# A 1 MB weight piece loaded by sixteen DMAs of 8 partitions instead of one of 128

## The chip, the cores and the metric

The kernel runs on one core of one Trainium2 chip. The metric is the device time in microseconds (us) of one execution; several executions are timed and their median is compared. TensorE (PE) multiplies matrices, VectorE (DVE) and ScalarE (ACT) work on elements, and SyncE (SP) here does nothing but issue DMAs, which sixteen DMA engines carry out.

## The reference

One layer of a decoder with 256 tokens of width 1024, all in float32. What matters here is its mixture of experts, which takes most of the time and nearly all of the data:

```python
def moe_ffn(h, w_router, b_router, w1, b1, w2, b2):      # 32 experts, top 4
    ...
    def expert_block(acc, xs):
        tok, g, e = xs
        u = jnp.dot(h_pad[tok], w1[e], ...) + b1[e]       # w1[e]: 1024 x 2048, 8 MB
        y = jnp.dot(clamped_swiglu(u), w2[e], ...) + b2[e]  # w2[e]: 1024 x 1024, 4 MB
        return acc.at[tok].add(y * g[:, None]), None
```

Before it stand the input projection, four retention heads, eight attention heads and the output projection; behind it a last RMS normalisation.

## The kernel before

Every expert's weights are read once from HBM: 32 x 12 MB. At most 64 tokens of an expert are taken at a time; on the inputs here one round over the experts is enough. SP loads the weights into `ring`, an SBUF buffer of 24 slots of 1 MB (128 partitions of 2048 floats each), used as 12 pairs. A piece of 2 MB fills a pair: row p of it is one contiguous stretch of HBM and goes to partition p. SP issues the loads in the order of use and holds each back with a wait on `chunk_used` until TensorE is through with what stood in the pair before. In the middle of the kernel two pieces are one DMA of 4 MB (`load_two`, L453).

TensorE works through step j: `up` multiplies the rows of expert j by its first layer, four pieces of 2 MB (L1477); `down` and its kin multiply the activations of expert j - 1 by its second layer, two pieces of 2 MB (L1500). `LAST` is expert 31, and step `E` = 32 has only the second layer of expert 31. SP and TensorE meet at semaphores: each DMA adds 16 when it has landed, and TensorE waits for the sum.

Near the end the pieces are cut finer, so that TensorE can begin on the first half of a piece while the second is on its way. `END_HALVES` names three pieces, the two of expert 30's second layer and the first of expert 31's; `load` brings each by two DMAs of 1 MB. L463 loads the first half with semaphore `half_in`, for which `down_first` waits; L464 loads the second half with `pair_full`, for which `down_rest` waits. The last piece of all comes in three DMAs (L460) of 1 MB, 512 KB and 512 KB, with semaphores `last_in`, for which `end_step` waits. Behind the last matmuls with weights stand `combine` (L1446), a sum of squares on ScalarE and VectorE, and the store of the output.

Of the kernel before, what the change touches and what calls it, by code (L numbers as in the profile page):

```python
# [23 lines left out]
P = 128  # L24
SEQ = 256
T = SEQ // P
D = 1024
# [21 lines left out]
W1_CHUNKS = C // 2  # L49
# [7 lines left out]
LAST = E - 1  # L57
BIAS_STEP, RESID_STEP, READ_STEP = 14, 20, 22
LAST_PARTS = [(0, 2), (2, 3), (3, 4)]
END_HALVES = [(LAST, W1_CHUNKS), (LAST, W1_CHUNKS + 1), (E, 0)]  # L60
assert PEEL + ITERS * UNROLL + 2 == E and TURNS * PAIRS == UNROLL * STEP_CHUNKS
SENTINEL = 3.0e38
LT_BANK, LOGIT_BANK = (3, 0), (2, 6)
# [32 lines left out]
def local_expert(i, j):  # L96

    return i * UNROLL + j
# [7 lines left out]
def down_chunk(j, k):  # L106

    return k if j == E else k - W1_CHUNKS
# [7 lines left out]
def pair_of(j, k):  # L116

    return place_in_stream(j, k) % PAIRS
# [27 lines left out]
def layer_kernel(nc, x, norm1_w, w_in, ret_norm_w, w_out, norm2_w, w_router, b_router,  # L146
# [9 lines left out]
    with ctx:  # L156
# [3 lines left out]
        def sem(name):  # L160
            return ctx.enter_context(nc.semaphore(name))
# [4 lines left out]
        def bank(b, n=1):  # L166
            return PS[:, b * BANK:(b + n) * BANK]
# [106 lines left out]
        last_in = [sem(f"last_in{k}") for k in range(len(LAST_PARTS))]  # L274
        half_in = [sem(f"half_in{k}") for k in range(len(END_HALVES))]
        pair_full = [sem(f"pair_full{d}") for d in range(PAIRS)]
# [135 lines left out]
        def _(sp):  # L412
# [14 lines left out]
            for j, pair in enumerate(WOUT_ORDER):  # L427
                s = WIN_CHUNKS + j
                dst = ring[:, s, :].rearrange("p (c n) -> p c n", c=2)
# [10 lines left out]
            def w1_half(e, k):  # L440

                return w1_v[e, k // 2, :, (k % 2) * 2 * SLOT_COLS:(k % 2 + 1) * 2 * SLOT_COLS]

            def w2_half(e, h):

                return w2_v[e, :, h * 2 * SLOT_COLS:(h + 1) * 2 * SLOT_COLS]
# [8 lines left out]
            def load(r, i, j, k):  # L455
                e, d = local_expert(i, j), pair_of(j, k)
                dst = ring[:, 2 * d:2 * d + 2, :].rearrange("p a n -> p (a n)")
                if j == E and k == W2_CHUNKS - 1:
                    for part, (a, b) in enumerate(LAST_PARTS):
                        sp.dma_start(dst[:, a * D:b * D], w2_half(e - 1, k)[:, a * D:b * D]).then_inc(last_in[part], 16)  # L460
                elif (j, k) in END_HALVES:
                    src = w2_half(e - 1, down_chunk(j, k))
                    sp.dma_start(dst[:, 0:2 * D], src[:, 0:2 * D]).then_inc(half_in[END_HALVES.index((j, k))], 16)  # L463
                    sp.dma_start(dst[:, 2 * D:], src[:, 2 * D:]).then_inc(pair_full[d], 16)  # L464
                elif j < E and k < W1_CHUNKS:
                    sp.dma_start(dst, w1_half(e, k)).then_inc(pair_full[d], 16)
                else:
                    sp.dma_start(dst, w2_half(e - 1, down_chunk(j, k))).then_inc(pair_full[d], 16)

            for g in FIRST_ORDER:  # L470
                if g == 10:
                    sp.wait_ge(decayed_ready, RET_HEADS)
                    sp.wait_ge(chunk_used, WIN_CHUNKS)
                elif g == 11:
                    sp.wait_ge(probT_ready, MOBA_HEADS)
                    sp.wait_ge(pv_done, 4)
                    sp.wait_ge(ret_done, RET_HEADS)
                    for v in range(2):
                        sp.dma_start(b1_sb[v * E:(v + 1) * E, :], b1[0, :, v * F:(v + 1) * F]).then_inc(late_in, 16)
                    sp.dma_start(b2_sb, b2[0, :, :]).then_inc(late_in, 16)  # L480
                    sp.wait_ge(gated, T)
                elif g == 8:
                    sp.wait_ge(retT_done, 2)
                elif g == 9:
                    sp.wait_ge(retT_done, 2)
                    sp.wait_ge(chunk_used, HEAD_CHUNKS - 2)
                else:
                    sp.wait_ge(chunk_used, min(2 * g + 2, HEAD_CHUNKS))
                if g == MOVED:
                    d = pair_of(0, g)  # L490
                    sp.dma_start(ring[:, 2 * d, :], w1_half(0, g)[:, 0:SLOT_COLS]).then_inc(pair_full[d], 16)
                    sp.dma_start(ring[:, 2 * d + 1, :], w2_half(1, 1)[:, SLOT_COLS:]).then_inc(ahead_in, 16)
                elif g < W1_CHUNKS:
                    load(0, 0, 0, g)
                else:
                    load(0, 0, 1 + (g - W1_CHUNKS) // STEP_CHUNKS, (g - W1_CHUNKS) % STEP_CHUNKS)
# [25 lines left out]
            def step_loads(r, i, j):  # L522
                for k in range(step_chunks(j)):
                    g = place_in_stream(j, k)
                    if doubled(j, k):
                        if k % 2:
                            sp.wait_ge(chunk_used, r * ROUND_CHUNKS + i * (UNROLL * STEP_CHUNKS)
                                       + (HEAD_CHUNKS + g - PAIRS + 1))
                            load_two(i, j, k - 1)
                        continue  # L530
                    if isinstance(r, int) and g == AHEAD:
                        load_ahead_rest(j, k)
                        continue
                    if isinstance(r, int) and g - PAIRS in CUTS:
                        load_cut(j, k, g - PAIRS)
                        continue
                    if g < PAIRS:
                        if isinstance(r, int):
                            continue

                        sp.wait_ge(chunk_used, r * ROUND_CHUNKS + HEAD_CHUNKS)
                    else:

                        sp.wait_ge(chunk_used, r * ROUND_CHUNKS + i * (UNROLL * STEP_CHUNKS)
                                   + (HEAD_CHUNKS + g - PAIRS + 1))
                    load(r, i, j, k)
# [570 lines left out]
        def _(pe):  # L1117
# [376 lines left out]
            def down_part(j, k, c0, c1, aT_n, out):  # L1494

                d, h = pair_of(j, k), down_chunk(j, k)
                for c in range(c0, c1):
                    for half in range(2):
                        cols = (c % 2) * D + half * BANK
                        last = mm(out[64 * half:64 * half + 64, :], aT_n[:, c, 64 * h:64 * h + 64],  # L1500
                                  ring[:, 2 * d + c // 2, cols:cols + BANK],
                                  start=(h == 0 and c == 0), stop=(h == 1 and c == 3))
                return last
# [14 lines left out]

            def down_first(r, j, k):

                pe.wait_ge(half_in[END_HALVES.index((j, k))], 16 * (r + 1))
                aT_n, out = (aT_last, bank(1)) if j == E else (aT, bank(5))
                down_part(j, k, 0, 2, aT_n, out)

# [13 lines left out]
            def last_step(r, i):  # L1538
                n = r * E + LAST
                pe.wait_ge(gh_ready, n + 1)  # L1540
                up(r, i, LAST, False)
                pe.wait_ge(put_ready, n)
                pe.wait_ge(actT_ready, n)
                down_first(r, LAST, W1_CHUNKS)
                down_rest(r, i, LAST, W1_CHUNKS)
                turn_act(n, bank(4))
                put_transposes(n + 1, bank(0))
                down_first(r, LAST, W1_CHUNKS + 1)
                down_rest(r, i, LAST, W1_CHUNKS + 1)

            def end_step(r, i):
                n = r * E + E
                pe.wait_ge(actT_ready, n)
                down_first(r, E, 0)
                pe.wait_ge(y_ready, n - 1)
                combine(putb, y_sb, (0,))
                down_rest(r, i, E, 0)
                for part, (c0, c1) in enumerate(LAST_PARTS):
                    pe.wait_ge(last_in[part], 16 * (r + 1))
                    last = down_part(E, 1, c0, c1, aT_last, bank(1))  # L1560
                last.then_inc(chunk_used, 1)
                combine(putb, y_sb, (1,))
                pe.wait_ge(put_ready, n)
                pe.wait_ge(y_ready, n)
                combine(put_last, y_last, (0, 1))
# [116 lines left out]
```

## Time and profile before

| | before |
|---|---|
| median of 3 runs | 1048.02 us (1047.65 to 1048.06) |
| span of the profiled execution | 1047.2 us |
| PE busy | 1028.6 us, 98% of the span |
| HBM traffic over the span | 405 GB/s |
| data moved by SP's queue | 423.51 MB |

The span runs from the first to the last instruction of one execution that was profiled; no other time stands on the page for that execution. It is 0.8 us below the median, which takes in what lies around the span. In the views, PE is a matmul and PEld the load of its weights; SPq is SP's DMA queue, the issue of DMAs. The DMA share of a window is the mean busy share of the sixteen DMA engines, and GB/s is what they moved. A TensorE instruction on 64 rows is printed by the profile as one with 128*64.

### The profile page before, as it was taken

How to read it: one execution, taken by the hardware profiler on the slowest of the kernel's cores; microseconds unless marked ns; L12 is line 12 of the kernel's file. 1: busy time of each engine (PE TensorE's matmuls, PEld its weight loads, DVE VectorE, ACT ScalarE, POOL GpSimd, SP SyncE). 2: the span in 40 equal slices, each digit the busy share in tenths (PEclk: the TensorE clock that was granted, in tenths of full speed). 3: DMA queues.
4: the chain of work that ended last, by engine and by line, in shares of the span. 5: the costliest groups of instructions: out<-in, count | busy, mean ns of one | idle time of the engine just before them, and what ended most of it. 6: DMA issues, size and time to landing. Idle time of an engine off the chain costs nothing.

```text
span 1047.2 us, 11219 instructions
## 1 busy us (share of the span) xinstructions
PE 1028.6 (98%) x4918; PEld 417.3 (40%) x4918; DVE 221.6 (21%) x584; ACT 117.5 (11%) x223; POOL 0.2 (0%) x4
## 2 busy tenths in 40 slices
PE   9999999999999999999999999999999999999996
PEld 7888543333333333333333333333333333333332
DVE  2174442111111111111111111111111111111111
ACT  2031121000000000000000000000000000000002
POOL 0000000000000000000000000000000000000000
PEclk9999999999999999999999999999999999999999
DMA  9992899999999999999999999999999999999995
GB/s 319 368 370 81 331 367 412 414 428 425 435 434 427 432 429 434 429 434 429 432 431 429 434 427 432 430 435 429 429 431 429 432 430 432 431 429 426 428 422 223
DMA packets 35958, 424.62 MB, mean 405 GB/s; under 512 B 3160, under 2 KB 15968, under 8 KB 19392
## 3 DMA queue, kind: packets, MB, share of 16 engines
q1 hardware_dynamic: 35600, 423.51, 96.2%
q8 instruction: 41, 0.67, 0.3%
q10 hardware_dynamic: 304, 0.33, 0.1%
q14 instruction: 13, 0.11, 0.0%
HBM read 422.78 MB, written 1.05 MB: 405 GB/s over the span
## 4 chain that ended last, share of the span: by engine, by line
PE 89%; DMA 9%; SPq 1%; another core or an unknown queue 0%; DVE 0%; issue 0%; ACT 0%; DVEq 0%; ACTq 0%
PE PS L1477 38%; PE PS L1500 19%; DMA ring<-in_w 9%; PE PS L1146 8%; PE PS L1446 5%; PE PS L1428 5%; PE PS L1325 3%; PE PS L1283 3%; PE PS L1535 2%; PE PS L1438 2%; PE PS L1420 1%; DMA ring<-in_w_in 1%; SPq L464 0%; PE PS L1608 0%; PE PS L1622 0%
## 5 line engine op out<-in xcount | busy, mean ns | idle before, releaser
L1477 PE MATMUL PS<-ring,work 128*64 128x512 f32 x1976 | 434.0, 596 | 5.7 <-DMA ring<-in_w 5.2
L1477 PEld LDWEIGHTS PS<-ring,work 128*64 128x64 f32 x1976 | 139.5, 137 | 277.2 <-issue 266.8
L1500 PE MATMUL PS<-ring,work 128*64 128x512 f32 x1024 | 227.6, 595 | 1.6 <-DMA ring<-in_w 1.6
L1500 PEld LDWEIGHTS PS<-ring,work 128*64 128x64 f32 x1024 | 72.2, 137 | 154.1 <-issue 149.0
L1035 DVE TENSOR_SCALAR work<-PS 128x512 f32<-128x512 f32 x32 | 22.1, 692 | 385.4 <-PE PS L1477 385.4
L1146 PE MATMUL PS<-ring 128*128 128x256 f32 x384 | 85.4, 380 | 1.4 <-DMA ring<-in_w_in 1.4
L669 ACT ACTIVATE work<-work 128x512 f32<-128x512 f32 x32 | 20.2, 630 | 523.5 <-DVE work L1035 523.5
L1146 PEld LDWEIGHTS PS<-ring 128*128 128x128 f32 x384 | 72.0, 190 | 11.9 <-DMA ring<-in_w_in 1.8
L1000 DVE TENSOR_TENSOR work<-PS,n2w 128x512 f32<-128x512 f32 x30 | 20.8, 692 | 228.5 <-PE PS L1438 228.5
L1446 PE MATMUL PS<-late,work 64*128 64x512 f32 x248 | 61.9, 616 | 0.0
L1428 PE MATMUL PS<-resid,work 128*64 128x512 f32 x248 | 58.5, 592 | 0.0
L686 ACT ACTIVATE late<-PS 128x512 f32<-128x512 f32 x30 | 17.9, 597 | 209.7 <-PE PS L1500 209.7
L1325 PE MATMUL PS<-work 32*64 32x512 f32 x256 | 35.8, 613 | 0.0
L1428 PEld LDWEIGHTS PS<-resid,work 128*64 128x64 f32 x248 | 17.9, 137 | 35.3 <-issue 35.3
L1008 DVE COPY work<-PS 128x256 f32<-128x256 f32 x31 | 13.2, 425 | 83.1 <-PE PS L1420 83.1
L1446 PEld LDWEIGHTS PS<-late,work 64*128 64x128 f32 x248 | 21.2, 186 | 19.4 <-issue 15.8
L1438 PEld LDWEIGHTS PS<-cst,work 128*128 128x128 f32 x124 | 17.3, 209 | 25.2 <-issue 25.2
L1535 PE MATMUL PS<-cst,work 128*128 128x128 f32 x128 | 23.9, 309 | 0.5
L1438 PE MATMUL PS<-cst,work 128*128 128x128 f32 x124 | 23.2, 309 | 0.0
L1039 DVE SCALAR_TENSOR_TENSOR work<-work 128x512 f32<-128x512 f32 x32 | 22.2, 693 | 3.3
L1042 DVE TENSOR_TENSOR work<-work 128x512 f32<-128x512 f32 x32 | 22.1, 692 | 1.1
L1036 DVE TENSOR_SCALAR work<-PS 128x512 f32<-128x512 f32 x32 | 21.8, 681 | 0.0
(176 smaller groups left out, 385.7 us busy)
## 6 DMA issues: line engine op xcount, KB each, us to landing
ring<-in_w SPq DMA_DIRECT2D x72, 4096.0 KB, 35.1
ring<-in_w SPq DMA_DIRECT2D x35, 2048.0 KB, 13.7
ring<-in_w SPq DMA_DIRECT2D x22, 1024.0 KB, 8.5
ring<-in_w_in SPq DMA_DIRECT2D x11, 1024.0 KB, 12.0
ring<-in_w_out SPq DMA_DIRECT2D x4, 1024.0 KB, 12.1
ring<-in_w SPq DMA_DIRECT2D x6, 512.0 KB, 6.9
ring<-in_w_in SPq DMA_DIRECT2D x2, 512.0 KB, 7.3
ring<-in_consts SPq DMA_DIRECT2D x1, 800.0 KB, 12.2
```

Source lines behind the costliest of these rows:

```text
L1035: nc.vector.tensor_scalar(g_sb, gate_bank, LIMIT, None, ALU.min).then_inc(gate_ready, 1)
L1039: nc.vector.scalar_tensor_tensor(a_sb, a_sb, 1.0, g_sb, ALU.add, ALU.mult).then_inc(glin_ready, 1)
L1042: nc.vector.tensor_tensor(a_sb, a_sb, s_sb, ALU.mult).then_inc(act_ready, 1)
L1146: last = mm(bank(4 + j % 2)[:, t * WIN_COLS:(t + 1) * WIN_COLS], hT[:, t, c, :], w[:, c, :], start=(c == 0), stop=(c == C - 1))
L1283: return mm(bank(2 + 4 * t + j), mixT(c)[:, t * P:(t + 1) * P], w[:, c % 2, j * BANK:(j + 1) * BANK], start=(c == 4), stop=(c == 3))
L1325: last = mm(bank(b0 + v)[64 * half:64 * half + 64, :], sel[v * E:(v + 1) * E, :], turned_half(b1_sb[v * E:(v + 1) * E, :], half), start=st ...
L1428: last = mm(bank(4)[64 * half:64 * half + 64, :], pick[:, t, :], resid[:, t, half_cols(half)], start=(t == 0), stop=(t == T - 1))
L1438: last = nc.tensor.transpose(bank(4)[:, c * P:(c + 1) * P], gx_v[:, c, :], ident)
L1446: last = mm(bank(2 + 4 * t + half), put[rows, t * P:(t + 1) * P], y[rows, :], start=start, stop=False, skip_group_check=True)
L1477: last = mm(bank(b0 + v)[64 * half:64 * half + 64, :], rows[:, c, :], turned_half(w[:, v * F:(v + 1) * F], half), start=(second and c == 0 ...
L1500: last = mm(out[64 * half:64 * half + 64, :], aT_n[:, c, 64 * h:64 * h + 64], ring[:, 2 * d + c // 2, cols:cols + BANK], start=(h == 0 and ...
L1535: last = nc.tensor.transpose(out[:, c * P:(c + 1) * P], a_v[:, c, :], ident)
```

## The change

The first half of the first piece of expert 30's second layer, step (LAST, W1_CHUNKS), is no longer one DMA with 128 rows of 8 KB but sixteen DMAs with 8 rows of 8 KB each. They add to the same semaphore, and TensorE waits for sixteen times as much before it begins on the piece. Source, destination and place in SP's program are the same, and all other loads too.

```diff
+STRIP = 8
+STRIPS = P // STRIP
+IN_STRIPS = (LAST, W1_CHUNKS)
@@ load
                 elif (j, k) in END_HALVES:
                     src = w2_half(e - 1, down_chunk(j, k))
-                    sp.dma_start(dst[:, 0:2 * D], src[:, 0:2 * D]).then_inc(half_in[END_HALVES.index((j, k))], 16)
+                    full = half_in[END_HALVES.index((j, k))]
+                    if (j, k) == IN_STRIPS:
+                        for a in range(0, P, STRIP):
+                            sp.dma_start(dst[a:a + STRIP, 0:2 * D], src[a:a + STRIP, 0:2 * D]).then_inc(full, 16)
+                    else:
+                        sp.dma_start(dst[:, 0:2 * D], src[:, 0:2 * D]).then_inc(full, 16)
                     sp.dma_start(dst[:, 2 * D:], src[:, 2 * D:]).then_inc(pair_full[d], 16)
@@ down_first
-                pe.wait_ge(half_in[END_HALVES.index((j, k))], 16 * (r + 1))
+                loads = STRIPS if (j, k) == IN_STRIPS else 1
+                pe.wait_ge(half_in[END_HALVES.index((j, k))], 16 * loads * (r + 1))
```

SP's program at the end of the weights, before. The first row is the four pieces of expert 31's first layer, and the two behind it are the halves of the piece in question; 128x4096 floats are 2 MB and 128x2048 are 1 MB.

```order
L466 DMA ring<-in_w 128x4096 [waits chunk_used] x4
L463 DMA ring<-in_w 128x2048 [waits chunk_used]
L464 DMA ring<-in_w 128x2048
L463 DMA ring<-in_w 128x2048 [waits chunk_used]
L464 DMA ring<-in_w 128x2048
L463 DMA ring<-in_w 128x2048 [waits chunk_used]
L464 DMA ring<-in_w 128x2048
L460 DMA ring<-in_w 128x2048 [waits chunk_used]
L460 DMA ring<-in_w 128x1024 x2
```

The same place in the changed kernel, where the lines have moved down by 3 to 8:

```order
L474 DMA ring<-in_w 128x4096 [waits chunk_used] x4
L469 DMA ring<-in_w 8x2048 [waits chunk_used]
L469 DMA ring<-in_w 8x2048 x15
L472 DMA ring<-in_w 128x2048
L471 DMA ring<-in_w 128x2048 [waits chunk_used]
L472 DMA ring<-in_w 128x2048
L471 DMA ring<-in_w 128x2048 [waits chunk_used]
L472 DMA ring<-in_w 128x2048
L463 DMA ring<-in_w 128x2048 [waits chunk_used]
L463 DMA ring<-in_w 128x1024 x2
```

One row of 1 MB has become sixteen instructions of 64 KB; eight larger DMAs stand behind them in the queue as before. TensorE's program at the place where the piece is used is the same in both, but for the value waited for, which these rows don't show. Here are the changed kernel's rows:

```order
L1485 MATMUL PS<-ring,work 64x512 [waits pair_full7]
L1485 MATMUL PS<-ring,work 64x512 x7
L1508 MATMUL PS<-ring,work 64x512 [waits half_in0,actT_ready,put_ready]
L1508 MATMUL PS<-ring,work 64x512 x3
L1508 MATMUL PS<-ring,work 64x512 [waits pair_full8]
L1508 MATMUL PS<-ring,work 64x512 x3
```

So nothing moves on TensorE; the wait for `half_in0` now ends with the last of sixteen landings.

## Rows read from the trace of the kernel before

**Rows 1.** The page: busy time by engine, and HBM traffic
```profile
PE 1028.6 (98%) x4918; PEld 417.3 (40%) x4918; DVE 221.6 (21%) x584; ACT 117.5 (11%) x223; POOL 0.2 (0%) x4
...
HBM read 422.78 MB, written 1.05 MB: 405 GB/s over the span
```

**Rows 2.** Windows: length, PE, PEld, DVE, ACT, POOL busy, PEclk, DMA share, GB/s
```profile
300.00:900.00 600.00, 597.63 (x2814) 208.87 (x2812) 103.95 (x238) 52.04 (x86) 0.00 (x0) 1.00 1.00 431
980.00:1010.00 30.00, 29.98 (x146) 10.48 (x144) 4.31 (x8) 2.42 (x4) 0.00 (x0) 1.00 1.00 427
```

**Rows 3.** Chain that ended last, from 983 us: start, us, what
```profile
987.51 40.83 DMA ring<-in_w
1028.34 0.14 issue
1028.47 1.94 PE PS L1500 x8
1030.41 1.06 PE PS L1446 x4
1031.47 5.49 PE PS L1500 x24
1036.96 2.83 PE PS L1446 x12
```

**Rows 4.** Timeline of TensorE's weight loads that waited for a DMA
```profile
1015.03 0.20 PEld L1477 LDWEIGHTS PS<-ring,work 128*64 128x64 f32 x4 [1.11 <-DMA ring<-in_w]
...
1026.05 0.20 PEld L1500 LDWEIGHTS PS<-ring,work 128*64 128x64 f32 x4 [2.05 <-DMA ring<-in_w]
...
1035.81 0.28 PEld L1500 LDWEIGHTS PS<-ring,work 128*64 128x64 f32 x4 [0.58 <-DMA ring<-in_w]
```

**Rows 5.** Windows over the last weight loads, columns as in rows 2
```profile
1020.00:1024.00 4.00, 4.00 (x22) 1.77 (x22) 1.83 (x4) 0.69 (x2) 0.00 (x0) 1.00 1.01 416
...
1028.00:1029.00 1.00, 0.53 (x4) 0.30 (x6) 0.00 (x0) 0.94 (x2) 0.00 (x0) 1.00 0.98 401
1029.00:1030.00 1.00, 1.00 (x8) 0.27 (x4) 0.00 (x0) 0.99 (x2) 0.00 (x0) 1.00 0.68 283
1030.00:1031.00 1.00, 1.00 (x6) 0.30 (x4) 0.00 (x0) 0.15 (x1) 0.00 (x0) 1.00 0.61 254
1031.00:1032.00 1.00, 1.00 (x8) 0.32 (x6) 0.00 (x0) 0.00 (x0) 0.00 (x0) 1.00 0.55 217
1032.00:1033.00 1.00, 1.00 (x8) 0.17 (x4) 0.00 (x0) 0.00 (x0) 0.00 (x0) 1.00 0.56 221
1033.00:1034.00 1.00, 1.00 (x6) 0.34 (x6) 0.00 (x0) 0.00 (x0) 0.00 (x0) 1.00 0.51 209
1034.00:1035.00 1.00, 1.00 (x6) 0.29 (x4) 0.00 (x0) 0.00 (x0) 0.00 (x0) 1.00 0.45 184
1035.00:1036.00 1.00, 1.00 (x8) 0.34 (x6) 0.00 (x0) 0.00 (x0) 0.00 (x0) 1.00 0.14 57
```

**Rows 6.** Timeline of SP's queue: start, us in the issue, line
```profile
970.37 4.23 SPq L463 DMA_DIRECT2D ring<-in_w  x1
...
987.51 0.44 SPq L463 DMA_DIRECT2D ring<-in_w  x1
988.00 12.93 SPq L464 DMA_DIRECT2D ring<-in_w  x1
1000.97 11.88 SPq L460 DMA_DIRECT2D ring<-in_w  x3
```

**Rows 7.** Line L463 by itself, issue to landing
```profile
DMA to landing us min/median/max: 40.8/43.5/47.1
```

**Rows 8.** Line L479, two loads of 32 partitions, 128 KB each
```profile
L479 SPq DMA_DIRECT2D work<-in_b x2: 336/376/415, 112.0 to 112.4; - x2
...
DMA to landing us min/median/max: 7.5/7.6/7.7
```

**Rows 9.** A window in which these loads are carried out, columns as above
```profile
118.40:118.90 0.50, 0.50 (x2) 0.19 (x1) 0.50 (x3) 0.00 (x0) 0.00 (x0) 1.00 1.00 213
```

**Rows 10.** The page's only load of 8 rows, and its issue on ScalarE's queue
```profile
work<-in_norm_w ACTq DMA_DIRECT2D x1, 4.0 KB
...
L567 ACTq DMA_DIRECT2D work<-in_norm_w x1: 584/584/584, 1.2 to 1.2; - x1
```

## The prediction

> **What bounds the kernel now.** I read the page first. TensorE is busy 98% of the span and the DMAs move 405 GB/s over all of it [rows 1], so either could be the bound. The windows decide it. From 300 to 900 us the share of busy time of the sixteen DMA engines is 1.00 at 431 GB/s, and from 980 to 1010 us still 1.00 at 427 [rows 2]; TensorE's 98% is a matmul that follows close behind the data. The chain of waits says the same for the end: it goes back from the last matmuls into a DMA of 40.83 us that lands at 1028.34 us and was issued at 987.51 [rows 3]. From 1015 to 1036 us TensorE stands at weights that are not there: 1.11 us at 1015.03, 2.05 at 1026.05, 0.58 at 1035.81 for the last piece [rows 4]. So the last landing, at 1035.8 us, sets the end, and 11.4 us of work follow it up to 1047.2. What delays the queue of loads at its end delays the kernel one for one; what brings the last landing forward helps as long as TensorE has idle time to give back, about 1.11 + 2.05 + 0.58 = 3.7 us by rows 4, of which a part is the ordinary gap of a weight load.
>
> The second thing to see is how the loads end. The sixteen engines don't finish together. Their share falls from 0.98 at 1028 us to 0.68, 0.61 and 0.55, stays at 0.56 and 0.51 until 1034, and is 0.14 in the last window [rows 5]. About half of them run dry between 1029 and 1031.5 us, the other half work on until about 1035.5. A DMA with 128 rows gives every engine 8, so all have carried the same load of it; one half is 4 to 6 us ahead of the other, and a piece lands when the laggards are through.
>
> The third is SP. Before the piece in question its issues take 4.23 us each, and the last ones 12.93 and 11.88 [rows 6]: it is held by a full queue, not by TensorE. The piece is issued at 970.37 us and lands 47.1 us later, at 1017.5 [rows 6, 7]. That is 20 MB of queue in front of it at 427 GB/s.
>
> **The change part by part.** The sum is made against the profiled execution, 1047.2 us of span; the median is 1048.0, so 0.8 us are added.
>
> SP. Fifteen instructions more. The only load of 8 rows in the trace took 0.58 us to issue [rows 10], so sixteen take about 9.3 us where one took 4.2. Behind them 47 us of queue are the cover, so I cost this at nothing; if the cover is gone, it is 5 us. But SP's queue is full at some limit that I can't read: 47.1 us of landing time over 4.9 us for a 2 MB piece at 427 GB/s is 9.6 DMAs. If the limit is a number of DMAs, sixteen small ones take the places of sixteen large ones, the queue behind them is short of work, and up to 2 or 3 us are lost while it is refilled at 0.4 to 0.6 us an issue [rows 6, 10].
>
> Bytes per engine. 1 MB at 427 GB/s is 2.45 us, eight rows of 8 KB on each engine, 0.31 us a row. A DMA of 8 rows can keep at most eight engines busy if a row isn't cut. The trace hints that it isn't: of the load of 8 rows the page gives no landing time [rows 10], though it has one for every load with 16 or more, which it takes from sixteen signals. If each strip goes to the same eight engines, these carry 16 rows, 4.9 us, and the others none. The eight are then 2.45 us later than before and the others 2.45 us earlier, a shift of 4.9 us between the halves, about what lies between them now.
>
> The Trainium skill (DMA: Bandwidth & Descriptors, section "Why a DMA increments its semaphore by 16 and not by 1") states that such a load runs on as many engines as divide its slowest dimension, the lowest-numbered ones: eight for 8 rows. The missing landing time agrees. By that rule alone the shift of 4.9 us holds; no row says whether the lowest-numbered are the early half.
>
> Which half it is: no view names the engines. I take the early half as the likelier, 7 to 3, as a judgement and not a reading. With no other cost, the early half would run dry 2.45 us later, its slowest at 1031.5 + 2.45 = 1034.0, and the laggards 2.45 us earlier, at 1033.3. The last landing would be at 1034.0 instead of 1035.8: **1.8 us gained**. On the lagging half it is 2.45 us lost.
>
> Where the rows go. The trace has two loads to 32 partitions, issued at 112.0 and 112.4 us and landed 7.5 and 7.7 us later [rows 8], 0.6 us apart for 128 KB. In the window in which they pass, the engines are busy 1.00 and move 213 GB/s [rows 9], half of the 427 to 431 that they move with the same share into 128 partitions [rows 2]. So 32 partitions take in only 213 GB/s, however many engines bring it. If that goes by the number of neighbouring partitions, 8 take 53 GB/s: a strip of 64 KB lasts 1.2 us, and sixteen in a row 19.7 us instead of 4.9. They needn't be in a row. The engines of a half stand up to 2 us apart [rows 5], so each is at another strip and other partitions. The bounds are 4.9 us (never two in the way of each other) and 19.7 us (always all). Between them I take two at a time, 0.61 us a row and 9.8 us in all, since that is the case of rows 9, where sixteen engines share room for eight. The eight engines are then 9.8 - 2.45 = 7.35 us later than before. Against this stands the lead of the slowest of them, 1035.8 - 1031.5 = 4.3 us. The last landing comes 7.35 - 4.3 = **3.05 us later**.
>
> The Trainium skill (SBUF — State Buffer, section "Door 1: The DMA port swizzle") has this as ports, sixteen in all, where 8 neighbouring partitions reach two. It would give 4 engines on each port for a strip, 1.2 us, the same as from rows 9. Rows 9 agree with it: 32 neighbours are eight ports, half of the rate. This rule speaks against the change, whatever half the strips fall on.
>
> TensorE. Nothing is added but a larger count to wait for. The piece now landed at 1017.5 us and is used from 1018 on, so a later landing stops TensorE at once, and all behind it is late by as much; that is the same delay as at the end, not a second one.
>
> Sum: 1047.2 + 0.8 + 3.05 = 1051.05, I say 1051.1.
>
> **The rivals.**
> Forecast: early half, rows in each other's way about two at a time. 1051.1, from 1049.5 (less in the way) to 1054 (more, or some refill of the queue). Chance 0.42.
> Faster: early half, and rows seldom in each other's way. Its place is the last landing, its price 1.8 us gained: 1046.2. It decides if the eight engines need less than 2.45 + 4.3 = 6.75 us for the sixteen strips. For it: the even fit of 4.9 us of shift to the lead. Against it: rows 9. Chance 0.27.
> Lagging half with rows in the way: their 7.35 us come with no lead, 1055.4. Chance 0.10. Lagging half without: 1050.5, chance 0.06.
> The strips follow one another, or the queue runs dry behind them: 19.7 - 6.75 = 13 us at the most, 1061; half of that is 1055 to 1058. For it: issues held for 4 to 13 us [rows 6]. Chance 0.08.
> The change doesn't do what it says, since rows are cut over all engines: 1048.0. Against it the missing landing time. Chance 0.07.
> That the load is hidden anyway I don't count: DMA engines are never idle before 1028 us [rows 2, 5].
>
> **How the numbers follow.** A change of 0.2%, 2.1 us, is about what a measurement of this kernel tells from none. The faster case lies at -1.8 with room to -2.4, so 0.09 of its 0.27 go beyond, and 0.18 are "same", with the 0.07 of no effect and 0.03 of the forecast's lower edge: 0.28. Slower has the rest, 0.63. For 8 in 10 the range runs from the faster case, 1046.0, to 1056.0, which leaves out its lower edge and the upper cases, some 0.15. As cases of both signs are in it: the forecast's own range is 1049.5 to 1054.
>
> **What would show it.** Right: in the windows after the last issue the share no longer falls to 0.5 for five windows; TensorE waits at the first L1508 for `half_in0` (before, it didn't), by 2 to 6 us; in the window of the strips GB/s is well under 427 at a share near 1.00. The faster case: no such wait, last landing 1034, share near 1 until 1033. The lagging half: share near 0.5 for longer than before. The queue: share well under 1.00 right behind the strips, and SP free again with issues of 0.4 us. Wrong in the main if the strips show no loss of rate, since the 7.35 us hang on one window of 0.5 us.

## The result and the profile after

The kernel became slower: 1056.24 us (median of 4 runs, 1055.39 to 1056.9) against 1047.95 us (1047.65 to 1048.06) for the kernel before in the same comparison. The ratio is 1.0079, with a 95% interval of 1.0067 to 1.0091, so 8.3 us more. The forecast was 1051.1 with a range of 1046 to 1056: the sign was right, the size was not. The profiled execution has a span of 1054.9 us, 7.7 more than before.

The page after, busy time by engine and the memory's traffic, as in [rows 1]:

```profile
PE 1030.2 (98%) x4918; PEld 416.8 (40%) x4918; DVE 221.5 (21%) x584; ACT 117.6 (11%) x223; POOL 0.2 (0%) x4
...
HBM read 422.78 MB, written 1.05 MB: 402 GB/s over the span
...
ring<-in_w SPq DMA_DIRECT2D x16, 64.0 KB
```

The same bytes and the same instructions on TensorE. The only new line is that of the sixteen strips, and again there is no landing time for them, as there was none for the one load of 8 rows before [rows 10].

The timeline of SP's queue after, columns as in [rows 6]; L469 are the strips, L471 the other first halves, L472 the second halves, L463 the last piece:

```profile
959.26 9.71 SPq L474 DMA_DIRECT2D ring<-in_w  x2
969.01 21.85 SPq L469 DMA_DIRECT2D ring<-in_w  x16
990.90 0.55 SPq L472 DMA_DIRECT2D ring<-in_w  x1
991.50 3.63 SPq L471 DMA_DIRECT2D ring<-in_w  x1
995.17 4.22 SPq L472 DMA_DIRECT2D ring<-in_w  x1
```

The strips held SP for 21.85 us where one issue had taken 4.23. Behind them there was still a queue: the next issues again take 3.6 to 4.2 us each, which is the sign of a full one.

Windows after, columns as in [rows 2]: length, busy time of five engines, PEclk, DMA share, GB/s. A DMA packet counts whole in the window in which it starts, so a share can stand above 1.00.

```profile
1005.00:1007.00 2.00, 2.00 (x12) 0.73 (x10) 0.00 (x0) 0.00 (x0) 0.00 (x0) 1.00 1.12 414
1007.00:1009.00 2.00, 2.00 (x13) 0.60 (x10) 0.00 (x0) 0.00 (x0) 0.00 (x0) 1.00 0.92 225
1009.00:1011.00 2.00, 2.00 (x12) 0.59 (x10) 0.00 (x0) 0.00 (x0) 0.00 (x0) 1.00 1.06 250
1011.00:1013.00 2.00, 2.00 (x12) 0.59 (x10) 0.00 (x0) 0.00 (x0) 0.00 (x0) 1.00 1.03 238
1013.00:1015.00 2.00, 0.62 (x4) 0.00 (x0) 0.00 (x0) 0.00 (x0) 0.00 (x0) 1.00 1.08 221
1015.00:1017.00 2.00, 0.00 (x0) 0.00 (x0) 0.00 (x0) 0.00 (x0) 0.00 (x0) 1.00 0.92 209
1017.00:1019.00 2.00, 0.21 (x2) 0.21 (x4) 0.00 (x0) 0.00 (x0) 0.00 (x0) 0.90 0.91 254
1019.00:1021.00 2.00, 2.00 (x6) 0.56 (x6) 0.00 (x0) 0.00 (x0) 0.00 (x0) 0.50 1.08 295
1021.00:1023.00 2.00, 2.00 (x10) 0.52 (x8) 0.00 (x0) 0.00 (x0) 0.00 (x0) 0.75 0.96 270
1023.00:1025.00 2.00, 1.02 (x6) 0.13 (x2) 0.93 (x2) 0.21 (x1) 0.00 (x0) 1.00 1.08 295
```

This is the picture to remember. The DMA engines stay busy, with a share near 1.00 in each window, and move 209 to 295 GB/s where they moved 414 two microseconds earlier. Nothing is idle and nothing is queued wrongly: the same transfers take longer, about twice as long up to 1017 us and one and a half times as long up to 1026. One row over 20 us each, for the kernel before and after, gives the sum:

```profile
1007.00:1027.00 20.00, 18.60 (x90) 6.18 (x88) 3.10 (x5) 1.23 (x2) 0.00 (x0) 1.00 1.01 419
```

```profile
1007.00:1027.00 20.00, 11.84 (x47) 3.21 (x42) 2.67 (x4) 0.63 (x1) 0.00 (x0) 0.91 1.00 258
```

At 258 instead of 419 GB/s, 20 us are worth 12.3, so 7.7 us are lost in this stretch, of the 8.3 in all.

TensorE's weight loads that waited, the answer to [rows 4], columns as there:

```profile
1018.79 0.29 PEld L1485 LDWEIGHTS PS<-ring,work 128*64 128x64 f32 x4 [6.06 <-DMA ring<-in_w]
...
1027.07 0.23 PEld L1508 LDWEIGHTS PS<-ring,work 128*64 128x64 f32 x4 [3.94 <-issue]
...
1043.98 0.33 PEld L1508 LDWEIGHTS PS<-ring,work 128*64 128x64 f32 x4 [0.53 <-DMA ring<-in_w]
```

The first long wait is 6.06 us at L1485, an up projection: that piece stands ahead of the strips in the queue and is a plain 128-row load, and it is late too. The next, 3.94 us, is at the first L1508, the matmuls that use the strips; the view names "issue", since it has no landing for them. The last wait for a DMA ends at 1043.98 where it ended at 1035.81 before: 8.2 us later. From there to the end it is 10.9 us, against 11.4 before. So the end is still set by the last landing, as the prediction had it.

The trace also has the time of every engine's signal to the semaphore of a load, which no view prints; these landing signals are read below by their times and spacing, since they don't name the engine either. The last of the strips' signals stands at 1026.97 us, right before the matmuls begin. From 1021 us on they come at the pace of two engines. Of the load that landed last, fourteen signals were there by 1040.4 us and two came at 1043.3 and 1043.9. So two engines that were late already and had strips set the end, 3.6 us behind the rest. Their way there has two parts. The load ahead of the strips was through at 1018.75 us instead of 1014.99: 3.8 us late, with no strip of their own behind them yet. Then their sixteen rows of strips took 8.2 us where eight rows had taken 2.5: 5.7 us more.

### The profile page after: what moved, and what is told of

The parts are those of the page before. It is cut to its first block, busy times and chain, and to the rows that moved or that the text cites. A ratio compares the mean times of both kernels' runs of the same rounds, so it can differ in the third digit from the quotient of the medians.

```text
span 1054.9 us, 11234 instructions
## 1 busy us (share of the span) xinstructions
PE 1030.2 (98%) x4918; PEld 416.8 (40%) x4918; DVE 221.5 (21%) x584; ACT 117.6 (11%) x223; POOL 0.2 (0%) x4
## 4 chain that ended last, share of the span: by engine, by line
PE 87%; DMA 9%; SPq 3%; DVE 0%; another core or an unknown queue 0%; issue 0%; ACT 0%; DVEq 0%; ACTq 0%
PE PS L1485 38%; PE PS L1508 19%; DMA ring<-in_w 8%; PE PS L1154 8%; PE PS L1454 5%; PE PS L1436 5%; PE PS L1333 3%; PE PS L1291 3%; PE PS L1544 2%; PE PS L1446 2%; SPq L469 2%; PE PS L1428 1%; DMA ring<-in_w_in 1%; SPq L472 0%; SPq L471 0%; PE PS L1617 0%
## 5 line engine op out<-in xcount | busy, mean ns | idle before, releaser
L1485 PE MATMUL PS<-ring,work 128*64 128x512 f32 x1976 | 435.6, 598 | 10.6 <-DMA ring<-in_w 10.1
L1485 PEld LDWEIGHTS PS<-ring,work 128*64 128x64 f32 x1976 | 139.8, 138 | 283.3 <-issue 267.6
L1508 PE MATMUL PS<-ring,work 128*64 128x512 f32 x1024 | 227.9, 596 | 4.1 <-DMA ring<-in_w 4.0
L1508 PEld LDWEIGHTS PS<-ring,work 128*64 128x64 f32 x1024 | 71.7, 137 | 157.5 <-issue 152.7
```

Of the source, the lines that this page charges most:

```text
L1485: last = mm(bank(b0 + v)[64 * half:64 * half + 64, :], rows[:, c, :], turned_half(w[:, v * F:(v + 1) * F], half), start=(second and c == 0 ...
```

## The experiments

Twelve kernels were run. e1 to e4 and e11 load the whole piece in another way; e6 to e10 and e12 load half of it, and e5 none, so their output isn't the reference's; the kernel before ran again on the same chip each time, at 1047.82, 1047.58 and 1047.79 us for the three groups (e1 to e4, e5 to e8, e9 to e12). In the diffs, `-` is the loop of the changed kernel.

My first theory was still that of the prediction: neighbouring partitions are in each other's way. The rival to it was that a small DMA costs by itself.

**e1: the rows of a strip 4 apart**

```diff
-    sp.dma_start(dst[a:a + STRIP, 0:2 * D], src[a:a + STRIP, 0:2 * D]).then_inc(full, 16)
+    rows = slice(a // 32 * 32 + a % 32 // STRIP, a // 32 * 32 + 32, 4)
+    sp.dma_start(dst[rows, 0:2 * D], src[rows, 0:2 * D]).then_inc(full, 16)
```

> The same piece in sixteen DMAs of 8 rows on the same engines, but the rows of a DMA go to partitions 4 apart instead of neighbours. Theory: the strips load eight engines with 16 rows each, two of which are laggards (the last five windows of the changed kernel show a DMA share of 0.12 to 0.22, two or three engines of sixteen), and neighbouring partitions take rows in slowly. Then only the 2.45 us of doubled load are left on the laggards: 1050.5 (1049.5 to 1051.5). Rival, the doubled load and the many issues alone cost it, whatever the partitions: 1055 to 1057 as before.

Measured: 1055.5 us, ratio 1.0073 (1.0056 to 1.009), 7.7 us over before, as the rival had it. Spacing the rows is no cure. But the windows were no longer slow from the start on, and by the landing signals the first eight strips, which go to partitions 0 to 63, landed quickly and the last eight slowly. That led to e6 and e7.

**e2: sixteen DMAs of 128 rows, 512 B each**

```diff
+    for a in range(0, 2 * D, P):
+        sp.dma_start(dst[:, a:a + P], src[:, a:a + P]).then_inc(full, 16)
```

> Sixteen DMAs again, each 64 KB, but each has all 128 partitions and 512 bytes of every row, so all sixteen engines carry the same. Theory: neither a doubled load nor crowded partitions, 1048 to 1049.5 (short rows may cost up to 1 us). Rival, the number of DMAs fills SP's queue and starves the engines: 1052 to 1056.

Measured: 1049.73 us, ratio 1.0018 (1.0009 to 1.0028), 1.9 us over before. As many DMAs as in the change, a quarter of its cost, and just over the range of the theory. Its loss is of another kind, as SP's queue and a window show:

```profile
969.09 44.98 SPq L469 DMA_DIRECT2D ring<-in_w  x16
1014.12 0.43 SPq L472 DMA_DIRECT2D ring<-in_w  x1
1014.59 0.43 SPq L471 DMA_DIRECT2D ring<-in_w  x1
```

```profile
1010.00:1012.00 2.00, 2.00 (x12) 0.65 (x10) 0.00 (x0) 0.00 (x0) 0.00 (x0) 1.00 0.59 238
1012.00:1014.00 2.00, 1.72 (x10) 0.49 (x8) 0.00 (x0) 0.00 (x0) 0.00 (x0) 1.00 0.75 227
```

Here SP is held for 45 us, until 1014.07, though the first of these loads land from 1006.9 on; the issues behind them take 0.43 each, so the queue isn't full any more, and the DMA share falls to 0.59. That is what a queue run dry looks like. The GB/s are as low as in the change, but only the share tells the two apart: few transfers under way, or all of them slow.

**e3 and e4: eight DMAs of 16 rows, neighbouring or 8 apart**

```diff
+    for a in range(0, P, 16):                                              # e3
+        sp.dma_start(dst[a:a + 16, 0:2 * D], src[a:a + 16, 0:2 * D]).then_inc(full, 16)
+    for a in range(8):                                                     # e4
+        sp.dma_start(dst[a::8, 0:2 * D], src[a::8, 0:2 * D]).then_inc(full, 16)
```

> Eight DMAs of 16 neighbouring partitions, one row for each of sixteen engines: no doubled load, but crowded partitions. Theory: if room goes by neighbours, 16 partitions take 107 GB/s, the piece 9.8 us instead of 2.45 in the worst case: 1051 to 1055. Rival, only the load on eight engines counts: 1048.

> Eight DMAs of 16 rows again on all engines, rows at partitions 8 apart. If any spacing relieves the crowd: 1048 to 1048.5. If the groups of partitions repeat after 32, as the ports of the Trainium skill do (SBUF — State Buffer, Door 1: eight groups reached by such a set, two rows each), up to 2.45 us more than that: 1049 to 1050.5. If spacing doesn't matter, the same as the eight DMAs of 16 neighbours.

Measured: 1054.51 us, ratio 1.0061 (1.0044 to 1.0078), and 1054.39, 1.0062 (1.0046 to 1.0079). With 16 rows all sixteen engines have work, as with 128 rows, and still 6.7 us are lost. So the uneven load of the engines is not what costs most, and spacing has no say here either.

After these four runs the theory had to change. The new one: in a 128-row load each engine's rows go to a place of the SBUF of its own, and a row that goes to another engine's place is what costs. The Trainium skill (DMA: Bandwidth & Descriptors, section "The descriptor swizzle") gives the places: engine 0 has partitions 0 to 3 and 32 to 35, engine 1 the next four of each, and so on to 63; engines 8 to 15 have 64 to 127 in the same way. No view names the engines; e6, e7 and e10 below agree with it by their times (-0.2, +6.1 and +3.5 us). If an 8-row strip runs on the first eight engines, one row after the other, then with rows 4 apart it is in place between 0 and 63 and out of place above. That order of the rows is an assumption that these times bear out and no trace shows. e5 leaves the piece out; e6 to e8 change where eight such strips go, and e8 also what they read.

**e5: without the piece** (TensorE doesn't wait for it either)

```diff
-    for a in range(0, P, STRIP): ...
+    pass
```

> The strips are left out and nothing takes their place: the last but one expert's first half piece isn't loaded, and TensorE multiplies by what the buffer held (that part of the output is then not the reference's). It gives the price of the 1 MB by itself. Both theories: 1 MB less at 427 GB/s is 2.45 us, so 1045.5, if the end stays bound by the loads. From here up is what the strips really cost: 1056.2 - 1045.5 = 10.7 us.

Measured: 1045.94 us, ratio 0.9982 (0.9972 to 0.9991), 1.6 us under before, where 2.45 were expected. The loss of the change over this kernel is 10 us for 1 MB.

**e6: eight strips to partitions 0 to 63, rows 4 apart**

```diff
+    for a in range(8):
+        rows = slice(a // 4 * 32 + a % 4, a // 4 * 32 + 32, 4)
+        sp.dma_start(dst[rows, 0:2 * D], src[rows, 0:2 * D]).then_inc(full, 16)
```

> Only eight strips, to partitions 0 to 63, rows 4 apart; rows 64 to 127 of the piece aren't loaded (that part of the output isn't the reference's). Theory 1 (an engine is slowed where its row goes to a part of the SBUF that other engines are filling at that time, and in partitions 0 to 63 with this spacing each of the eight engines is at its own): eight rows on each of eight engines, the same as they carry of a 128-row DMA, at 0.31 us: 1048.0, the same as before, from 1047.0 to 1049.0. Theory 2 (each small DMA costs something by itself, wherever it goes): half of the strips, half of the loss over the kernel without the piece: 1045.5 + 5.4 = 1050.9.

**e7: the same to partitions 64 to 127**

```diff
+        rows = slice(64 + a // 4 * 32 + a % 4, 64 + a // 4 * 32 + 32, 4)
```

> The same eight strips with the same spacing, to partitions 64 to 127, rows 64 to 127 of the piece; rows 0 to 63 aren't loaded. Same engines, same bytes, same number of DMAs. Theory 1: each of the eight engines shares with one of the other eight, 0.55 to 0.61 us a row instead of 0.31, so 2 to 2.5 us or more later than with the strips to partitions 0 to 63: 1050.5 to 1052. Theory 2: the same as that kernel within 0.5 us.

Measured: e6 1047.42 us, ratio 0.9998 (0.9988 to 1.0008), the same as before; e7 1053.68, ratio 1.0061 (1.0044 to 1.0078). The two have the same number of DMAs, the same rows per DMA, the same spacing, the same bytes, and, by the row counts, the same engines. They stand 6.3 us apart; e7 is 1.7 us above what was expected of it. The rival, a cost of each small DMA, falls: e6 has eight of them and loses nothing. Windows of e6:

```profile
1007.00:1009.00 2.00, 2.00 (x12) 0.62 (x10) 0.00 (x0) 0.00 (x0) 0.00 (x0) 1.00 1.01 426
1009.00:1011.00 2.00, 2.00 (x12) 0.69 (x10) 0.00 (x0) 0.00 (x0) 0.00 (x0) 1.00 0.98 414
```

Windows of e7:

```profile
1007.00:1009.00 2.00, 2.00 (x12) 0.73 (x10) 0.00 (x0) 0.00 (x0) 0.00 (x0) 1.00 1.12 258
1009.00:1011.00 2.00, 1.18 (x6) 0.15 (x2) 0.00 (x0) 0.00 (x0) 0.00 (x0) 1.00 1.00 209
1011.00:1013.00 2.00, 0.82 (x4) 0.35 (x6) 0.00 (x0) 0.00 (x0) 0.00 (x0) 0.87 0.97 221
1013.00:1015.00 2.00, 2.00 (x8) 0.58 (x6) 0.00 (x0) 0.00 (x0) 0.00 (x0) 0.50 0.94 340
1015.00:1017.00 2.00, 2.00 (x10) 0.53 (x6) 0.00 (x0) 0.00 (x0) 0.00 (x0) 0.78 1.06 336
1017.00:1019.00 2.00, 0.60 (x6) 0.07 (x4) 0.00 (x0) 0.00 (x0) 0.00 (x0) 1.00 0.98 205
1019.00:1021.00 2.00, 2.00 (x10) 0.71 (x12) 0.00 (x0) 0.00 (x0) 0.00 (x0) 1.00 0.99 213
1021.00:1023.00 2.00, 2.00 (x12) 0.74 (x10) 0.36 (x1) 0.00 (x0) 0.00 (x0) 1.00 0.97 385
```

In e7 the rate falls to half, 205 to 221 GB/s, and not by a quarter, as it would if only the eight engines with strips went at half speed. And it does so twice, from 1007 to 1013 and from 1017 to 1021. The landing signals give the reason for the two dips: of the eight engines with strips six are among the early ones and two among the late ones, some 7 us behind. In the second dip only these two are at their strips. If each of them held up just the one engine whose place it uses, as the expectation had it, four of sixteen would go at half rate, and 14/16 of 427 would be left, 374 GB/s by estimate. 205 and 213 were moved. The single packets of the trace say the same: of those that start between 1017 and 1021 us, 8 KB took 0.62 us in the median and 19 in 20 took 0.53 or more; in e6 it was 0.31. So in these dips all sixteen engines are slow.

It isn't so always. Between the dips one engine, some 2 us behind the other early ones, is still at its strips, its signals 0.6 us apart. It is then nearly alone in being slow: 8 KB took 0.31 us in the median, and 94 in 100 took under 0.5.

```profile
1014.00:1015.00 1.00, 1.00 (x4) 0.24 (x2) 0.00 (x0) 0.00 (x0) 0.00 (x0) 0.50 0.92 369
1015.00:1016.00 1.00, 1.00 (x4) 0.24 (x2) 0.00 (x0) 0.00 (x0) 0.00 (x0) 0.56 0.97 377
```

Why the two slow all of them here and the one doesn't wasn't found.

**e8: to partitions 64 to 127, but reading the rows of memory of 0 to 63**

```diff
+        rows = slice(a // 4 * 32 + a % 4, a // 4 * 32 + 32, 4)
+        into = slice(64 + a // 4 * 32 + a % 4, 64 + a // 4 * 32 + 32, 4)
+        sp.dma_start(dst[into, 0:2 * D], src[rows, 0:2 * D]).then_inc(full, 16)
```

> Eight strips to partitions 64 to 127 again, but with the rows of memory that belong to partitions 0 to 63 (that part of the output isn't the reference's). Theory 1 (the SBUF's side decides): as the kernel with the strips to partitions 64 to 127, 1050.5 to 1052. Rival (the side of memory decides, which rows are read at the same time): as the kernel with the strips to partitions 0 to 63.

Measured: 1052.67 us, ratio 1.0046 (1.003 to 1.0063). It goes with e7 and not with e6, whose rows of memory it reads. So the side of the SBUF decides. The time is again above the range.

Three more kernels ask what "in place" means, and one asks how many engines it takes.

**e9: eight strips of neighbouring partitions, 0 to 63, and e10: e6 moved up by four partitions**

```diff
+    for a in range(0, 64, STRIP):                                          # e9
+        sp.dma_start(dst[a:a + STRIP, 0:2 * D], src[a:a + STRIP, 0:2 * D]).then_inc(full, 16)
+        rows = slice(4 + a // 4 * 32 + a % 4, 36 + a // 4 * 32 + a % 4, 4)  # e10
```

> Eight strips of 8 neighbouring partitions, 0 to 63, as the first half of the change makes them; rows 64 to 127 aren't loaded (that part of the output isn't the reference's). Theory 1 (only a row that goes to another engine's place in the SBUF slows the loads, and then all of them to half of their rate, as the windows of the strips to partitions 64 to 127 have it, 221 to 257 GB/s): of each strip's eight rows most go to another's place, so 1052 to 1054, with windows at 205 to 260 GB/s. Rival (partitions 0 to 63 are good for these engines however the rows are spaced): 1047.4, as with rows 4 apart, and windows at 410 to 425 GB/s.

> Eight strips of 8 rows 4 apart, moved up by four partitions, to 4 to 67; the others aren't loaded (that part of the output isn't the reference's). Spacing, engines and bytes are as in the kernel with partitions 0 to 63; all that changes is that each engine's row lands where the next engine's would. Theory 1: each row is in another's place, so the full loss, 1053 to 1054, at half rate for 8 to 12 us. Rival (the border at partition 64 decides, and only 4 of 64 rows are beyond it): 1047.4 to 1048.5.

Measured: e9 1051.27 us, ratio 1.0036 (1.0023 to 1.0048); e10 1051.33, ratio 1.0034 (1.002 to 1.0048). Both lose 3.5 us where e6 lost nothing. e10 is the neat one: it differs from e6 only in that each row lands four partitions further up, where the next engine's would. The rival of a border at partition 64 falls. But the loss is 3.5, where the ranges had 4.2 to 6.2 and 5.2 to 6.2. In e10 the first dip is as deep as in e7 and the second is not, as its windows show (1013 to 1015, where e7 also recovers, is left out):

```profile
1007.00:1009.00 2.00, 2.00 (x12) 0.68 (x10) 0.00 (x0) 0.00 (x0) 0.00 (x0) 1.00 1.01 221
1009.00:1011.00 2.00, 1.69 (x10) 0.39 (x8) 0.00 (x0) 0.00 (x0) 0.00 (x0) 1.00 1.01 209
...
1015.00:1017.00 2.00, 0.00 (x0) 0.00 (x0) 0.00 (x0) 0.00 (x0) 0.00 (x0) 0.82 1.02 266
1017.00:1019.00 2.00, 1.99 (x6) 0.76 (x8) 0.00 (x0) 0.00 (x0) 0.00 (x0) 0.50 1.00 377
```

So rows out of place within 0 to 63 slow all engines in the first dip and only some in the second. What makes the difference wasn't found.

**e11: the whole piece, e6 and one DMA of 64 rows for the upper half**

```diff
+        (the eight strips of e6)
+    sp.dma_start(dst[64:P, 0:2 * D], src[64:P, 0:2 * D]).then_inc(full, 16)
```

> Eight strips to partitions 0 to 63, rows 4 apart, and one DMA of 64 rows for partitions 64 to 127: the whole piece. If the DMA of 64 rows runs at full rate (all its rows in their engines' places): 8 engines carry 12 rows and 8 carry 4, two of the late ones 1.25 us more, so 1048 to 1049.5. If its rows are dealt to the engines without regard to the place, as the two loads to 32 partitions with 213 GB/s let expect: 64 rows over 16 engines, 4 a piece at 0.61 us, 2.5 us at half rate in each of the two stretches in which the strips to partitions 64 to 127 had 5, so some 3 us more, 1050.5 to 1052.

Measured: 1052.99 us, ratio 1.0053 (1.0036 to 1.007), 5.2 us over before. A single large DMA of 512 KB does this. Number and size of DMAs are out of it: of e6's eight small ones and this one, it is this one that costs. It was expected in place or out of place with 3 us more; it cost 2 us beyond that.

**e12: sixteen strips of 4 rows to partitions 64 to 127**

```diff
+    for a in range(16):
+        rows = slice(64 + a // 4 * 16 + a % 4, 64 + a // 4 * 16 + 16, 4)
+        sp.dma_start(dst[rows, 0:2 * D], src[rows, 0:2 * D]).then_inc(full, 16)
```

> Sixteen strips of 4 rows, 4 apart, to partitions 64 to 127; rows 0 to 63 aren't loaded (that part of the output isn't the reference's). Four engines carry 16 rows each where eight carried 8. Theory 1 in its strong form (one row in a wrong place anywhere halves the rate of all sixteen engines): 16 rows of 0.62 us are 10 us at half rate, 5 us lost, and four engines carry 2.45 us more; 1051 to 1054, and windows at 205 to 260 GB/s. Its weak form (only the engines slow that share a place, here four others): the windows stay at half of 430 for at most eight of sixteen engines, 320 GB/s or more.

Measured: 1054.96 us, ratio 1.0072 (1.0055 to 1.0089). Its windows:

```profile
1007.00:1009.00 2.00, 2.00 (x12) 0.73 (x10) 0.00 (x0) 0.00 (x0) 0.00 (x0) 1.00 1.13 307
1009.00:1011.00 2.00, 1.27 (x6) 0.15 (x2) 0.00 (x0) 0.00 (x0) 0.00 (x0) 1.00 1.03 234
1011.00:1013.00 2.00, 1.86 (x10) 0.72 (x12) 0.00 (x0) 0.00 (x0) 0.00 (x0) 1.00 0.93 209
1013.00:1015.00 2.00, 1.79 (x10) 0.34 (x6) 0.00 (x0) 0.00 (x0) 0.00 (x0) 1.00 1.11 246
1015.00:1017.00 2.00, 0.00 (x0) 0.00 (x0) 0.00 (x0) 0.00 (x0) 0.00 (x0) 1.00 0.97 221
1017.00:1019.00 2.00, 0.00 (x0) 0.00 (x0) 0.00 (x0) 0.00 (x0) 0.00 (x0) 1.00 0.86 299
1019.00:1021.00 2.00, 1.77 (x6) 0.61 (x8) 0.00 (x0) 0.00 (x0) 0.00 (x0) 0.61 1.04 393
```

Only four engines have strips, sixteen rows each, and the whole machine runs at about half rate in one dip of some 10 us, which is 16 rows of 0.61 us. Four engines at half speed, and four more that share a place with them, would have left 320 GB/s. The strong form of the theory holds in this dip: of the packets that start between 1008 and 1017 us, 19 in 20 took 0.53 us or more for 8 KB. From 1019 to 1021 us, when by the signals one engine alone is still at its strips, it doesn't hold: 393 GB/s. The time lies 1 us above the range of the strong form. By the table below 4.9 of the 7.2 us are in the windows. The landing signals show where more was lost: three of the four were through with the load ahead of the strips by 1008.1 us, and the fourth at 1011.9. It was at its sixteen rows until 1021.4, and its last landing, at 1040.4 us, came 3.2 us after the other fifteen.

All kernels side by side. "Lost" is 20 us times the share by which GB/s from 1007 to 1027 us falls short of the 419 of before.

| kernel | over before, us | GB/s | DMA share | lost, us |
|---|---|---|---|---|
| the change | +8.3 | 258 | 1.00 | 7.7 |
| e1 8 rows, 4 apart | +7.7 | 290 | 1.00 | 6.2 |
| e2 128 rows of 512 B | +1.9 | 341 | 0.89 | 3.7 |
| e3 16 rows, neighbours | +6.7 | 282 | 1.01 | 6.5 |
| e4 16 rows, 8 apart | +6.6 | 291 | 1.01 | 6.1 |
| e5 no piece | -1.6 | 408 | 0.99 | 0.5 |
| e6 in place | -0.2 | 412 | 1.00 | 0.3 |
| e7 out of place | +6.1 | 301 | 1.01 | 5.6 |
| e8 as e7, other source | +5.1 | 299 | 1.01 | 5.7 |
| e9 low, neighbours | +3.5 | 332 | 1.00 | 4.2 |
| e10 e6 moved by 4 | +3.5 | 338 | 1.00 | 3.9 |
| e11 e6 and 64 rows | +5.2 | 327 | 1.01 | 4.4 |
| e12 4 rows, out of place | +7.2 | 317 | 1.01 | 4.9 |

Kernels that load less have to gain by it: at 427 GB/s 2.45 us come off the last column for e5, which lacks 1 MB, and 1.2 for e6 to e10 and e12, which lack half of it. Then, where the share stays near 1.00, the loss of rate in this one stretch accounts for the time within 1 us, but for e1, e7 and e12, which are 1.5, 1.7 and 3.5 us slower than that. Nothing here points to a version that beats the kernel before: of those that load the whole piece the best, e2, is 1.9 us slower.

## Why the prediction was right or wrong

**The bound** was right. The last landing sets the end (shown by the waits): it moved by 8.2 us, the profiled span by 7.7 and the median by 8.3. TensorE and what follows gave back 0.5 us at most. That the DMA engines are "never idle before 1028 us" was read too widely: it holds in the windows shown, but the page has a slice near 90 us with a share of two tenths. Nothing hangs on it.

**SP at nothing** was right in effect, with a wrong size. Sixteen issues took 21.85 us and not 9.3, and the 47 us of queue covered them all. The queue's limit is not a number of DMAs, or the strips would have emptied it as e2's issues did. The rival of a queue run dry named 1055 to 1058, close to the result, but its sign, a share well under 1.00 behind the strips, isn't there.

**Bytes per engine** was right in kind: each 8-row strip has eight landing signals and no landing time. The rule of the Trainium skill (DMA: Bandwidth & Descriptors, section "Why a DMA increments its semaphore by 16 and not by 1") for the number of engines fits that. The two late engines needed 5.7 us more for sixteen rows than for eight before, where the sum had 7.35. "Early half, 7 to 3" was the wrong question: the landing signals make it six early engines and two late ones.

**The price of a row**, 0.61 us, held: e12's dip of 10 us for sixteen rows is 0.6 us a row. In the change itself it was 0.5 on the two late engines, 8.2 us for sixteen. It was read from [rows 9], and that window was the right one to look at. Its cause was read wrongly: I took the number of neighbouring partitions, with 53 GB/s for 8 of them. e6 against e9 and e10 shows that it is the place relative to the engine: strips 4 apart lose nothing in place, and 3.5 us moved by four partitions.

**The step that failed** is the last one: "Against this stands the lead of the slowest of them, 1035.8 - 1031.5 = 4.3 us. The last landing comes 7.35 - 4.3 = 3.05 us later." It makes two mistakes. It puts all strips on the early half, so that a lead pays for them; two of the eight engines are among the laggards, have no lead, and set the last landing. And it charges the slow rows only to the engines that carry them; the runs show that others are held up by them, in the dips of e7 and e12 all sixteen. e7 shows this second part alone, since its eight engines carry no more rows than before: 6.1 us. In the change it is the 3.8 us by which the two late engines came to their strips too late, while the early ones were at theirs. With the 5.7 us of their own rows that is 9.5 us at the end of the strips, of which 8.2 are left at the last landing; where the rest went stays open. The sum had 7.35 - 4.3 = 3.05. That the two parts are those of the change is read from its landing signals; no run took one of them away with all else left as it was.

The same mistake in small: a piece ahead of the strips landed 3.8 us late, and TensorE waited 6.06 us for it at L1485. The prediction looked only behind the strips, at the first L1508.

**The rivals.** "Lagging half with rows in the way", 1055.4, came nearest in time and was half right: laggards with strips and no lead set the end. But they were two and not eight, their rows cost 5.7 us and not 7.35, and the 3.8 us from the others' rows are not in it, so that its number came close is luck. The faster one, rows seldom in each other's way, is what happens to strips that are in place: e6 lost nothing. "Rows cut over all engines", 1048.0, falls with the eight signals of each strip.

**The range** missed by 0.24 us, and it had no case in which slow rows cost more than their own engines' time.

## What to carry to other kernels

Loads of 4, 8, 16 and 64 rows all cost time here in a stream of 128-row loads, unless each row landed where the engine puts its rows of a 128-row load anyway; while two or more engines had rows out of place, up to all sixteen ran at half rate. So expect up to half of the stretch to be lost, and count the stretch once for each group of engines that isn't in step; in the change itself the rate was half for 10 us and two thirds for 9 more. Then look which engine lands last, and whether it carries more than the others. In a profile look for GB/s at half with the DMA share at 1.00, and charge the loss to everything that is in flight, not to the transfer that causes it.

## What the runs showed of the hardware that was not expected

- Half rate can be common property: with four of sixteen engines out of place the core moved 209 to 246 GB/s, from 1009 to 1017 us (e12), where the kernel with all rows in place moved 414 to 426 (e6, 1007 to 1011 us). With one engine out of place it was 369 and 377 (e7). The Trainium skill (SBUF — State Buffer, section "Door 1: The DMA port swizzle") explains low rates by how many ports the partitions reach. By ports alone the two late engines of e7 would then hold up two others; the second dip shows more than this, and no run here shows by what way the others are held.
- The engines of a core are not in step. In the trace of before, the sixteen landing signals of one 128-row load stand up to 7.9 us apart. The distance grew through the run: 2.3 us near 340 us, 3.8 near 450, 5.4 near 750 and 7.0 near 970. After SP had let the queue run empty in e2 they were 0.7 to 2.3 us apart.
- One issue on SP with a full queue takes 4.2 us for a load of 128 rows, 1.18 us for a strip (the median of sixteen), and 2.8 us for 128 rows of 512 B (44.98 us for sixteen).
- TensorE's granted clock was 0.50, its lower level of 1.2 GHz, from 1019 to 1021 us, after it had stood idle from 1013.6 to 1018.8 waiting for a late piece. It was 1.00 again from 1023 on, and TensorE waited for the strips once more after that, so the end wasn't touched by it.
